# FFN up-projection: the narrow matmul of each output block placed right behind its wide one

## What is computed

```
def conv_ffn(h, w_up, conv_w, conv_b, w_down):
    z = dwconv(h @ w_up, conv_w, conv_b, FFN_CONV // 2)
    g, v = jnp.split(z, 2, axis=-1)
    return (jax.nn.silu(g) * v) @ w_down
```

## Time and profile before

| what | value |
|---|---|
| time, three runs | 2392.1, 2392.34 and 2392.46 us, median 2392.34 us |
| span of the profiled execution | 2390.1 us |
| what lies around the span (median less span) | 2.2 us |
| TensorE busy | 2371.8 us, 99% of the span |
| VectorE busy | 1632.4 us, 68% |
| ScalarE busy | 1167.6 us, 49% |
| wide stretches (lines 443 and 447) | 1645.7 to 1827.5, 1914.9 to 2094.5 and 2181.4 to 2316.2 us |

### The profile page before, as it was taken

How to read it: one execution, slowest core, us unless ns; L and a number is a source line. 1 busy time by engine, 2 the same in 40 slices (tenths; PEclk the granted TensorE clock), 3 DMA queues, 4 the chain that set the end, 5 groups by cost and what they waited for, 6 DMA issues and landing times.

```text
span 2390.1 us, 30519 instructions
## 1 busy us (share of the span) xinstructions
PE 2371.8 (99%) x11950; PEld 2016.7 (84%) x11950; DVE 1632.4 (68%) x2108; ACT 1167.6 (49%) x1499; POOL 0.2 (0%) x4
## 2 busy tenths in 40 slices
PE   9999999999999999999999999999999999999998
PEld 9989888888888888888888888888888888888887
DVE  5775657676776676687667777556777566765776
ACT  5443545534434434456554443446555355544554
POOL 0000000000000000000000000000000000000000
PEclk9999999999999999999999999999999999999999
DMA  7444566888888888875888887665555655566554
GB/s 264 154 161 152 200 196 251 278 282 294 275 283 290 280 286 280 287 260 182 304 292 288 284 291 270 222 205 164 189 185 194 193 186 189 190 190 191 189 182 157
DMA packets 153421, 550.37 MB, mean 230 GB/s; under 512 B 17984, under 2 KB 19776, under 8 KB 152384
## 3 DMA queue, kind: packets, MB, share of 16 engines
q1 hardware_dynamic: 152720, 548.06, 68.1%
q10 hardware_dynamic: 560, 0.36, 0.1%
HBM read 546.24 MB, written 2.11 MB: 229 GB/s over the span
## 4 chain that ended last, share of the span: by engine, by line
PE 96%; DVE 2%; ACT 1%; DMA 1%; issue 1%; DVEq 0%; ACTq 0%
PE bank L464 21%; PE bank L466 21%; PE bank L465 21%; PE bank L443 7%; PE mis L443 7%; PE mis L447 3%; PE bank L447 3%; PE bank L429 2%; PE bank L430 2%; PE bank L431 2%; PE mis L466 2%; PE mis L465 2%; PE mis L464 2%; PE mis L551 1%; PE mis L707 1%; DMA raw<-wstream 1%
## 5 line engine op out<-in xcount | busy, mean ns | idle before, releaser
L1209 DVE TENSOR_TENSOR wlo<-raw,whi 128x1024 fp32r<-128x1024 f32 x824 | 1004.5, 1224 | 689.3 <-ACT whi L790 688.5
L790 ACT ACTIVATE whi<-raw 128x1024 fp32r<-128x1024 f32 x824 | 869.0, 1059 | 1077.8 <-PE bank L466 673.2
L464 PE MATMUL bank<-whi,xs 128*128 128x512 f32 x1152 | 453.8, 394 | 1.1 <-issue 1.1
L466 PE MATMUL bank<-wlo,xs 128*128 128x512 f32 x1152 | 448.9, 390 | 0.0
L465 PE MATMUL bank<-whi,xs 128*128 128x512 f32 x1152 | 448.4, 389 | 0.0
L464 PE MATMUL bank<-whi,hs 128*128 128x512 f32 x1060 | 413.1, 390 | 1.6 <-DVE wlo L1209 1.6
L466 PE MATMUL bank<-wlo,hs 128*128 128x512 f32 x1060 | 412.5, 389 | 0.0
L465 PE MATMUL bank<-whi,hs 128*128 128x512 f32 x1060 | 412.4, 389 | 0.0
L466 PEld LDWEIGHTS bank<-wlo,xs 128*128 128x128 f32 x1152 | 216.2, 188 | 45.5
L464 PEld LDWEIGHTS bank<-whi,xs 128*128 128x128 f32 x1152 | 216.4, 188 | 44.9 <-issue 1.5
L465 PEld LDWEIGHTS bank<-whi,xs 128*128 128x128 f32 x1152 | 216.5, 188 | 43.5
(11 more groups left out here) (215 smaller groups left out, 2011.4 us busy)
## 6 DMA issues: line engine op xcount, KB each, us to landing
raw<-wstream SPq DMA_DIRECT2D x824, 512.0 KB, 4.3
aring<-astream SPq DMA_DIRECT2D x192, 512.0 KB, 5.0
gvb<-gvrow SPq DMA_DIRECT2D x8, 256.0 KB, 5.6
gate<-gate_rows SPq DMA_DIRECT2D x2, 1024.0 KB, 8.7
x<-xt SPq DMA_DIRECT2D x3, 512.0 KB, 8.6
out<-acc SPq DMA_DIRECT2D x2, 640.0 KB, 3.6
pw<-poolw SPq DMA_DIRECT2D x1, 1024.0 KB, 5.5
silu_c<-rows SPq DMA_DIRECT2D x1, 1024.0 KB, 5.3
```

The source lines that it names most:

```text
L464: pe.matmul(o, h, whi[:, slot, c], start=first and k == 0, stop=False)
L466: mm = pe.matmul(o, h, wlo[:, slot, c], start=False, stop=last and k == UK - 1)
L790: act.activation(whi[:, slot, :], raw[:, slot, :], ACT.Copy).then_inc(hi_ready, 1)
L1209: dve.tensor_tensor(wlo[:, slot, :], raw[:, slot, :], whi[:, slot, :].bitcast(F32), ALU.subtract).then_inc(lo_ready, 1)
```

## The change

The loop over `m` that issued four narrow matmuls behind four wide ones is merged into the loop that issues the wide ones. The matmuls, their operands, banks, start and stop flags and semaphores are the same, and each bank still sees them in the same order. Only the order across banks changes.

```
                     for m in range(MT):
                         c = slice(k * NC + m * P, k * NC + (m + 1) * P)
                         pe.matmul(banks[m][:, :], whi[:, slot, c], xs[:, kt0 + k, :], start=first and k == 0, stop=False,
                                   skip_group_check=True)
-                    for m in range(MT):
-                        c = slice(k * NC + m * P, k * NC + (m + 1) * P)
                         mm = pe.matmul(banks[m][:, 0:T], wlo[:, slot, c], xs[:, kt0 + k, 0:T], start=False,
                                        stop=last and k == UK - 1, skip_group_check=True)
                 mm.then_inc(unit_used, 1)
```

## The result

The changed kernel takes 2395.84 us in the median of 21 runs, the kernel before beside it 2392.39 us. The ratio is 1.0012, with a 95% interval of 1.0007 to 1.0018: some 3.5 us slower by the medians, within the 0.2% that the prediction called "same". The profiled execution spans 2393.8 us.

The account below looks back on a forecast made before the run. TensorE, 99% busy, was taken to bound the kernel through its matmul pitch. Loads, banks and fetches added 0 us, switches +1.0: 2390.1 + 1.0 = 2391.1 us span, plus 2.2 to the median, 2393.3 us; range 2386.0 to 2400.0.

Parts of the forecast that it names:

- The forecast case: Wide units: the excess stays about where it is, a pair between 347.4 and 354.2 ns, most likely 351.5; chance 0.42.
- two of the rivals: Wide units: alternation locks at 346.7 ns a pair (0.32), or the short matmul takes the disturbance, 356.0 ns (0.16).
- No wait stands in front of these units, so only TensorE's rhythm can change.: Wide units: TensorE is busy throughout, its only line-443 wait is 0.6 us, so only the matmul pitch can move.
- Loads keep their cover, banks and operands cost nothing.: Wide units: each load still runs beside a matmul, bank order and operands are harmless; 0 us each.
- The excess comes from the switch between lengths and has a memory.: Wide units: short-to-long switches cause 16.3 ns over the clean pitches per `k`, and the disturbance lasts into later matmuls.
- The size of the term.: Wide units: the alternating pair takes 351.5 ns, +0.7 ns over 1408 pairs, +1.0 us.
- The upper bound from single matmuls: Wide units: slowest wide matmul (398 ns) beside longest narrow one (283) bounds the pair at 356.0 ns, +7.3 us.
- The rival that it falls into step: Wide units: the alternation locks at the clean 346.7 ns a pair, -5.8 us, 2386.5 us; chance 0.32.
- The rival that each switch from short to long costs 16.3 ns: Wide units: four such switches per `k` instead of one add 17.2 us, giving 2409.5 us; chance 0.10.
- The skill's gap: Wide units: N/2.4 + 2.5 ns a matmul, 216 and 109 ns, so 325 ns a pair in either order, no change.

Follow-up runs that it names:

- half-load runs: Wide units with 64 stationary columns instead of 128 outside each group's first unit: changed order 340.0 ns a pair, runs of four 343.2, 512 columns everywhere 460.0.
- runs of two: Two wide then two narrow matmuls in a row, against four and four in the kernel before: 348.32 ns a pair, 3.44 us less, ratio 0.9984.
- pairs of 8, 16 and 32: That many wide, then narrow matmuls in a row, against four before: 349.16, 347.93 and 347.30 ns a pair; ratios 0.9990, 0.9989 and 0.9979.

## Why the prediction was right, and where it was off

The forecast case came about: the excess stayed about where it was, and the time within 0.2%. That alone says little: the range of 2386.0 to 2400.0 us also took in two of the rivals, the case itself had 0.42, and of the 3.5 us that the kernel lost the forecast had 1.0. Point by point:

- *No wait stands in front of these units, so only TensorE's rhythm can change.* Right. Busy time, clock and waits are as before, and 1408 pairs at +2.5 ns are the 3.5 us.
- *Loads keep their cover, banks and operands cost nothing.* Right for banks and operands, each shown by a run of its own at the same 353.3 ns. That no load lost its cover fits (no new wait appeared at lines 443 and 445), but "0 us" for the loads was argued and not shown: in the half-load runs the order's effect has the other sign.
- *The excess comes from the switch between lengths and has a memory.* Right with full loads. Equal lengths are clean in the changed order; the memory gave the pairs of 8, 16 and 32 ahead of their runs. It did not give runs of two.
- *The size of the term.* This is where it was off: I took 351.5 ns (+0.7, +1.0 us) as the middle of what the first wide and the first narrow matmul behind a switch have the earlier trace rows. Measured is 353.3 (+2.5, +3.5 us). A wide matmul that is always the first behind a switch has 403, 398 or 395 ns, on average 398.7 and not 396: the disturbance is carried from one to the next past the narrow one. By the pitches that is 236.0 against the 233.5 put down for it; the narrow one has 117.3 against 118.5 and 117.5. The predicted 2393.3 us was 2.5 us short.
- *The upper bound from single matmuls* (398 and 283, 356.0 ns) held for the pair, though single wide ones go to 403.
- *The rival that it falls into step* failed: the alternation does lock into a cycle, but into one of three pairs at 353.3 ns each, with no clean wide matmul among the 704 of `mis`. My argument for it, that the disturbance shows in the second to fourth wide matmul "which the new order never has", was wrong, and the earlier trace rows already spoke against it: the first wide one had 396 ns, 7 over the clean 389. The rival was not absurd: entered from half loads, the alternation ran one unit at the clean sum.
- *The rival that each switch from short to long costs 16.3 ns* failed: four switches in a `k` cost 4 x 6.6 = 26 ns, not 65, and two in a `k`, in runs of two, 2 x 3.3.
- *The skill's gap* (the Trainium skill, TensorE: Matmul & The Clock Gate, Back-to-back issue gap), which the skill gives for an isolated matmul; that it holds whatever stands beside it was the prediction's reading, and for a stream of loads and matmuls the same section has another figure, 131 ns at 512 columns. No run here has either: 512 columns take 226.7 ns, and seven orders of the same 1408 pairs give pairs from 347.3 to 353.3 ns, all above the 325 estimated from the skill's figures.

What stays open is the mechanism inside. The runs show that the pitch depends on the sequence of column counts, on the number of stationary columns and on the state at entry, and that it runs through fixed cycles (three pairs in the change). Whether the load and the stream compete for a read path, and what sets them back in step, no run here tells; the one simple model of it that was put to the test (13.3 ns a matmul, in proportion to the load) fell.

## What to carry to other kernels

When TensorE is never idle, look at the pitch from start to start and compare it with that of a long run of equal matmuls: what lies over it is a cost with no wait to its name. Where matmuls of two lengths alternate, longer runs of equal ones are worth trying; mirroring every second block doubles the run without holding anything more. Short runs are not ordered by length (two was better than one, three, four or even eight, and gave 3.4 of the 4.9 us that 32 gave), so they have to be tried. The whole prize here was 0.2% of the kernel, from pairs that fill a fifth of it.

## What the hardware showed that I had not expected

- A sequence of two lengths can stay in a disturbed cycle through all 64 units of a stretch, 1.2% (350.8) or 1.9% (353.3) over the clean 346.7 ns, while each length by itself, with full loads, settles at once or within some nine matmuls.
- Which cycle it takes depends on what ran before: the same alternation had 353.3 ns a pair behind token matmuls and 346.6 behind half loads.
- The excess of a turn is not monotonic in the run: 6.6, 3.3, 7.7, 16.4, 20, 20, 20 ns for runs of 1, 2, 3, 4, 8, 16 and 32.
- Matmuls with half the stationary columns can be slower: 230.0 against 226.7 ns at 512 columns, in a cycle of six matmuls.
